# One level product and one score matrix for both directions of a gated scan, in a whole-network kernel on Trainium2

## The reference

```python
def step(S, xs):
    qc, kc, vc, gc = xs
    b = jnp.cumsum(gc, axis=2)
    decay = jnp.exp(jnp.where(lower, b[:, :, :, None, :] - b[:, :, None, :, :], -jnp.inf))
    a = jnp.einsum('bhtk,bhtsk,bhsk->bhts', qc, decay, kc)
    o = jnp.einsum('bhts,bhsv->bhtv', a, vc) + jnp.einsum('bhtk,bhkv->bhtv', qc * jnp.exp(b), S)
    ...
o_f, s_fwd = chunked_gated_scan(q, k_f, v, lf_f, s_fwd)
o_b, s_bwd = chunked_gated_scan(q[:, ::-1], k_b[:, ::-1], v[:, ::-1], lf_b[:, ::-1], s_bwd)
return o_f + o_b[:, ::-1], s_fwd, s_bwd
```

## Time and profile before

| | before |
|---|---|
| median of 3 runs | 3801.09 us (3799.83 to 3802.03) |
| the profiled execution | 3799.04 us, span 3797.2 us |
| TensorE (PE) busy | 3507.4 us, 92% of the span |
| VectorE (DVE) | 1810.3 us, 48% |
| ScalarE (ACT) | 1262.7 us, 33% |
| GpSimd (POOL) | 359.3 us, 9% |
| granted TensorE clock, mean | 0.958 |
| scan stage | about 1229 to 1855 us of the span |

### The profile page before, as it was taken

How to read it: one execution, slowest core, us unless ns; L and a number is a source line. 1 busy time by engine, 2 the same in 40 slices (tenths; PEclk the granted TensorE clock), 3 DMA queues, 4 the chain that set the end, 5 groups by cost and what they waited for, 6 DMA issues and landing times.

```text
span 3797.2 us, 44325 instructions
## 1 busy us (share of the span) xinstructions
PE 3507.4 (92%) x17640; PEld 2915.7 (77%) x17640; DVE 1810.3 (48%) x2841; ACT 1262.7 (33%) x1955; POOL 359.3 (9%) x386
## 2 busy tenths in 40 slices
PE   4999988999998887888799999999989999999898
PEld 3777777888887776777678887887768778877686
DVE  4665657755524456655543333334333333343333
ACT  2444443212123344434332223333332333333322
POOL 1010011000001222322200000001100000001000
PEclk7999989999998998898799999999999999999999
DMA  4222203655621210110123322222212232222122
GB/s 166 81 59 66 64 22 100 196 190 197 192 78 47 65 40 29 39 39 23 39 92 95 95 89 96 72 73 83 73 51 94 88 99 70 72 84 72 51 97 86
DMA packets 108269, 319.30 MB, mean 84 GB/s; under 512 B 28192, under 2 KB 29728, under 8 KB 107552
## 3 DMA queue, kind: packets, MB, share of 16 engines
q1 hardware_dynamic: 108064, 316.46, 26.1%
HBM read 314.32 MB, written 2.10 MB: 83 GB/s over the span
## 4 chain that ended last, share of the span: by engine, by line
PE 83%; DVE 8%; ACT 4%; issue 3%; DMA 1%; POOL 0%; SPq 0%; DVEq 0%; ACTq 0%
PE bank L913 20%; PE bank L915 19%; PE bank L914 19%; PE bank L918 3%; PE bank L919 3%; PE bank L920 3%; PE bank L1049 3%; PE bank L998 1%; PE bank L1102 1%; DVE tmp L1540 1%; PE bank L1121 1%; PE bank L1131 1%; ACT L1159 1%; PE bank L986 1%; PE bank L1084 1%
## 5 line engine op out<-in xcount | busy, mean ns | idle before, releaser
L913 PE MATMUL bank<-h_high_lat,w_high 128*128 128x512 f32 x2752 | 1148.2, 417 | 68.8 <-DVE h_low_ctx L1546 35.6
L915 PE MATMUL bank<-h_high_lat,w_low 128*128 128x512 f32 x2752 | 1088.5, 396 | 0.0
L914 PE MATMUL bank<-h_low_lat,w_high 128*128 128x512 f32 x2752 | 1088.0, 395 | 0.0
L1494 DVE TENSOR_TENSOR w_low<-w_raw,w_high 128x1024 fp32r<-128x1024 f32 (+2 forms) x440 | 527.7, 1201 | 1138.2 <-ACT w_high L1179 1137.1
L1179 ACT CAST w_high<-w_raw 128x1024 fp32r<-128x1024 f32 (+2 forms) x440 | 451.0, 1027 | 1384.4 <-PE bank L915 861.1
L913 PEld LDWEIGHTS bank<-h_high_lat,w_high 128*128 128x128 f32 x2752 | 526.5, 191 | 187.2 <-issue 73.0
L915 PEld LDWEIGHTS bank<-h_high_lat,w_low 128*128 128x128 f32 x2752 | 525.6, 191 | 114.8
L914 PEld LDWEIGHTS bank<-h_low_lat,w_high 128*128 128x128 f32 x2752 | 527.9, 192 | 80.7 <-issue 8.2
L1506 DVE SCALAR_TENSOR_TENSOR ada_product<-w_raw,c_rows 128x1024 f32<-128x1024 f32 x192 | 246.5, 1284 | 63.9 <-DMA w_raw<-in_ada_w_dram 51.8
L918 PE MATMUL bank<-h_high_ctx,w_high 128*128 128x256 f32 x800 | 225.7, 282 | 0.0
L919 PE MATMUL bank<-h_low_ctx,w_high 128*128 128x256 f32 x800 | 225.4, 282 | 0.0
(11 more groups left out here) (250 smaller groups left out, 4512.0 us busy)
## 6 DMA issues: line engine op xcount, KB each, us to landing
w_raw<-in_w_in_dram SPq DMA_DIRECT2D x176, 512.0 KB, 3.5
w_raw<-in_ada_w_dram SPq DMA_DIRECT2D x88, 512.0 KB, 3.6
w_raw<-in_ffn_in_dram SPq DMA_DIRECT2D x88, 512.0 KB, 3.6
w_raw<-in_w_ada_dram SPq DMA_DIRECT2D x48, 512.0 KB, 4.4
w_raw<-in_hg_in_dram SPq DMA_DIRECT2D x40, 512.0 KB, 3.5
w_raw<-in_ffn_out_dram SPq DMA_DIRECT2D x32, 512.0 KB, 3.6
w_raw<-in_qkv_dram SPq DMA_DIRECT2D x24, 512.0 KB, 3.5
w_raw<-in_proj_ret_dram SPq DMA_DIRECT2D x16, 512.0 KB, 3.5
```

Source lines behind the costliest of these rows:

```text
L913: e.matmul(lat_b, a, h[:, k, :], start=start, stop=False)
L914: e.matmul(lat_b, a, l[:, k, :], start=False, stop=False)
L915: done = e.matmul(lat_b, b, h[:, k, :], start=False, stop=stop)
L1494: e.tensor_tensor(w_lo[n % 2][:, 0:w], raw[slot][:, 0:w], w_hi[n % 2][:, 0:w].bitcast(F32), ALU.subtract).then_inc(s_lo, 1)
```

## The change

The forward direction needs scores from an earlier to a later half of each block, the backward one from a later to an earlier half. The new `hg_x` therefore holds two 512-column parts: keys (forward keys in first halves, backward keys in second halves) and queries, each with its decay. One product of the two gives both directions' scores of a level, in 128 columns a chunk, and one mask takes both from it into one matrix `hg_a`. So there are seven levels where there were fourteen, each with four GpSimd differences (the same 256 columns), one exponential of 1024 columns, three multiplications (256, 256, 512), four 128-column products and one masked copy of 512 columns. The diagonal is made once, from the sum of the two key tensors (`hg_ks`, a new VectorE addition in `square1`), and `hg_o` multiplies `v` once. GpSimd's first level waits for both running sums. The masks are half as many and are loaded in two parts. The generator's parts are now 26, spread as if 24, so its last two come when the next head's starts, and `LAG`, `KHAT` and `STATE` are set anew.

```diff
-LAG = 5
-KHAT, STATE = (3, 9), (6, 12)
+LAG = 3
+KHAT, STATE = (2, 5), (4, 7)
...
             yield
-        jobs = [(d, li) for d in range(2) for li in range(len(LEVELS))]
-        for s in range(len(jobs) + LAG):
+        for s in range(len(LEVELS) + LAG):
             if s >= LAG:
-                self.ev("hg_a", i, *jobs[s - LAG])
-            if s < len(jobs):
-                self.ev("hg_df", i, *jobs[s])
-            if 1 <= s <= len(jobs):
-                self.ev("hg_fa", i, *jobs[s - 1])
+                self.ev("hg_a", i, s - LAG)
+            if s < len(LEVELS):
+                self.ev("hg_df", i, s)
+            if 1 <= s <= len(LEVELS):
+                self.ev("hg_fa", i, s - 1)
             if s == 1:
-                self.ev("hg_a", i, 0, -1)
-            if s == 8:
-                self.ev("hg_a", i, 1, -1)
...
-        self.interleave([self.hg_pieces(i) for i in range(HG_HEADS)], [(self.hg_mixer(i), 36) for i in range(HG_HEADS)], 5 * (KC - 1))
+        self.interleave([self.hg_pieces(i) for i in range(HG_HEADS)], [(self.hg_mixer(i), 24) for i in range(HG_HEADS)], 5 * (KC - 1))
...
-            hg_d = ring("hg_d", 2, [P, LAT], st)
-            hg_x = ring("hg_x", 4, [P, LAT], st)
+            hg_d = ring("hg_d", 2, [P, 2, LAT], st)
+            hg_x = ring("hg_x", 3, [P, 2, LAT], st)
+            hg_ks = sqr[1][:, 0:LAT]
...
-            hg_a = ring("hg_a", 2, [P, NCH, P], st)
+            hg_a = sb("hg_a", [P, NCH, P], F32, st)
...
                     e.dma_start(hg_reset[:, :], io["hg_reset"]).then_inc(s_reset, 16)
                     e.wait_ge(s_nl, low_before[2] + KC)
-                    for u in range(4):
-                        d, lo, n = u // 2, (0, 4)[u % 2], (4, 3)[u % 2]
-                        if u >= 2:
-                            e.wait_ge(s_hm, u - 1)
-                        words = tmp[u % 2][:, 0:n * P].bitcast(U32).rearrange("p (l t) -> p l t", t=P)
-                        e.dma_start(words, io["hg_masks"][:, d, lo:lo + n, :]).then_inc(s_hml[u % 2], 16)
+                    for u, (lo, n) in enumerate(((0, 4), (4, 3))):
+                        words = tmp[u][:, 0:n * P].bitcast(U32).rearrange("p (l t) -> p l t", t=P)
+                        e.dma_start(words, io["hg_masks"][:, lo:lo + n, :]).then_inc(s_hml[u], 16)
...
-                            done = e.matmul(b[:, cols], hg_k[(2 * i + d) % 3][:, cols], hg_q[i % 2][:, cols], start=True, stop=True)
+                            done = e.matmul(b[:, cols], hg_ks[:, cols], hg_q[i % 2][:, cols], start=True, stop=True)
                     else:
-                        job = NL * (2 * i + d) + li
-                        half = 1 - d
+                        job = NL * i + li
                         e.wait_ge(s_hx, job + 1)
                         for n in range(NCH):
-                            xs = hg_x[job % 4][:, n * P:(n + 1) * P]
-                            xt = xs.rearrange("p (b a s) -> p b a s", a=2, s=LEVELS[li])[:, :, half, :]
-                            done = e.matmul(b[:, n * P // 2:(n + 1) * P // 2], xs, xt, start=True, stop=True)
+                            cols = slice(n * P, (n + 1) * P)
+                            done = e.matmul(b[:, cols], hg_x[job % 3][:, 0, cols], hg_x[job % 3][:, 1, cols], start=True, stop=True)
                     done.then_inc(s_hpa, 1)
...
                         cols = slice(n * P, (n + 1) * P)
                         for d in range(2):
                             e.matmul(b[:, cols], hg_st[d][:, n, :], hg_qb[d][:, cols], start=d == 0, stop=False)
-                            done = e.matmul(b[:, cols], hg_vt[:, n, :], hg_a[d][:, n, :], start=False, stop=d == 1)
+                        done = e.matmul(b[:, cols], hg_vt[:, n, :], hg_a[:, n, :], start=False, stop=True)
                     done.then_inc(s_hgo, 1)
...
                         e.tensor_scalar(t[:, :], t[:, :], TINY, None, ALU.max).then_inc(s_hft, 1)
+                    if i > 0:
+                        e.wait_ge(s_ha, ha_last[i - 1])
+                    e.wait_ge(s_hkk, 2 * i + 2)
+                    e.tensor_tensor(hg_ks[:, :], hg_k[2 * i % 3][:, 0:LAT], hg_k[(2 * i + 1) % 3][:, 0:LAT], ALU.add).then_inc(s_hks, 1)
...
-                    if job >= 4:
-                        was, li4 = divmod(job - 4, NL)
-                        e.wait_ge(s_hpa, nth[("hg_a", was // 2, was % 2, li4)])
+                    _, i, li = ev
+                    job = NL * i + li
+                    x, dl = hg_x[job % 3], hg_d[job % 2]
+                    if job >= 3:
+                        e.wait_ge(s_hpa, nth[("hg_a", *divmod(job - 3, NL))])
                     e.wait_ge(s_hde, job + 1)
-                    e.tensor_tensor(xv[:, :, 0, :], dv[:, :, 0, :], s1[:, :, 0, :], ALU.mult)
-                    e.tensor_tensor(xv[:, :, 1, :], dv[:, :, 1, :], s2[:, :, 1, :], ALU.mult).then_inc(s_hx, 1)
+                    e.wait_ge(s_hkk, 2 * i + 2)
+                    for a in range(2):
+                        e.tensor_tensor(hg_half(x[:, 0, :], li, a), hg_half(dl[:, 0, :], li, a), hg_half(hg_k[(2 * i + a) % 3], li, a), ALU.mult)
+                    e.tensor_tensor(x[:, 1, :], dl[:, 1, :], hg_q[i % 2][:, :], ALU.mult).then_inc(s_hx, 1)
                 elif kind == "hg_a":
-                    _, i, d, li = ev
-                    b, at = mix_bank[(ev, 0)], hg_a[d]
+                    _, i, li = ev
+                    b = mix_bank[(ev, 0)][:, :].rearrange("p (n t) -> p n t", t=P)
...
-                            e.wait_ge(s_hm, 4)
-                        e.wait_ge(s_ha, hg_before[ev])
+                            e.wait_ge(s_hm, 2)
+                        e.wait_ge(s_ha, nth[ev] - 1)
                         e.wait_ge(s_hpa, nth[ev])
-                        e.copy_predicated(to, mk.unsqueeze(1).broadcast_to([P, NCH, P // 2 // m, m]),
-                                          b[:, 0:LAT // 2].rearrange("p (n b s) -> p n b s", n=NCH, s=m)).then_inc(s_ha, 1)
+                        e.copy_predicated(hg_a[:, :, :], hg_mask[:, li:li + 1, :].broadcast_to([P, NCH, P]), b).then_inc(s_ha, 1)
                 elif kind == "hg_rd":
...
+                    _, i, li = ev
+                    job, m = NL * i + li, LEVELS[li]
+                    dk, dq = hg_d[job % 2][:, 0, :], hg_d[job % 2][:, 1, :]
+                    blocks = [P, LAT // (2 * m), m]
+                    bf, bb = ([hg_half(hg_b[d], li, a) for a in range(2)] for d in range(2))
+                    ref_f = bf[0][:, :, m - 1:m].broadcast_to(blocks)
+                    ref_b = bb[1][:, :, 0:1].broadcast_to(blocks)
                     if li == 0:
-                        e.wait_ge(s_hb, 2 * i + d + 1)
+                        e.wait_ge(s_hb, 2 * i + 2)
                     if job >= 2:
                         e.wait_ge(s_hx, job - 1)
-                    e.tensor_tensor(dv[:, :, 0, :], *p1, ALU.subtract)
-                    e.tensor_tensor(dv[:, :, 1, :], *p2, ALU.subtract).then_inc(s_hd, 1)
+                    e.tensor_tensor(hg_half(dk, li, 0), ref_f, bf[0], ALU.subtract)
+                    e.tensor_tensor(hg_half(dq, li, 1), bf[1], ref_f, ALU.subtract)
+                    e.tensor_tensor(hg_half(dk, li, 1), ref_b, bb[1], ALU.subtract)
+                    e.tensor_tensor(hg_half(dq, li, 0), bb[0], ref_b, ALU.subtract).then_inc(s_hd, 1)
```

70 lines of the change are left out of this document (22 added, 48 removed).

## The result

| | before | after |
|---|---|---|
| median | 3801.56 us (4 runs, 3799.83 to 3806.07) | 3712.38 us (4 runs, 3711.68 to 3712.99) |
| profiled execution | 3799.0 us | 3712.8 us |
| one head, seven of them, sum | 525.3 us | 443.8 us |
| last value piece to the next stage's first weight subtraction | 62.3 us | 58.7 us |
| granted clock, mean | 0.958 | 0.966 |

The ratio is 0.9764, 95% interval 0.9747 to 0.978: 89 us saved, where I had forecast 99, a time of 3702 and a range of 3683 to 3730. The forecast holds, 10 us off its middle.

A forecast was written before the change was run, and what follows sets the result against it. TensorE, busy for 92% of the span, and its waits were taken to bound the kernel. Savings of 90 us in seven heads, 6 in the last scan and 3 at the stage's start sum to 99: 3702 us, range 3683 to 3730.

The forecast's parts named there:

- first part: Head up to its first level's product, set by the ScalarE, VectorE and GpSimd chain: from 25.6 to 28.0 us.
- second part: Head from its first level's product on, set by TensorE's own work: from 49.5 to 33.5 us at full clock.
- clock loss: Time lost in a head to the clock falling in TensorE's waits: 0.8 us, a value near the low end.
- seven heads: Scans beside the next head's weights: 62.3 us each, 12.8 less, 90 us saved for seven.
- last scan: The eighth scan, running alone: 6 us saved, with ends of 3 and 9.
- start of the stage: Two mask loads and no wait let the next weights issue earlier: 3 us saved, bounds 1 and 3.2.
- (5) of the first part: GpSimd starts after both scans and has two levels ready before ScalarE is free for them: costs nothing.
- the readout: Its product now comes two steps into the next head, so the sigmoids and the chain start 1.7 us later.
- the three multiplications: First level's operands on VectorE: two operations of 0.41 and one of 0.68 replace two of 0.41, 0.7 us more.
- The rival (low as long as now): Clock stays low after the first level: 2.3 us a head more, 16 in all, 3718 us; chance 20%.
- GpSimd's pace: GpSimd's 5.8 us a level sets the second part: 3770 us, chance 4%; or slower, about 3840, chance 3%.
- the price of columns: A 128-column level costs twice a 64-column one: 5.7 us more a head, 40 in all, 3742 us; chance 3%.

The follow-up runs named there:

- run 1: Changed kernel with the output product and readout's product two slots earlier, before the next head starts, as in the kernel before; 3705.69 us.
- run 8: Kernel before the change with the first direction's key transposes one slot later; 3805.63 us, a single run.
- run 3: Changed kernel with each level's four products made twice over, same results; 3754.54 us.
- run 5: Changed kernel with products nobody reads added ahead of TensorE's four waits in seven heads, to hold the clock up; 3703.39 us.
- run 4: Changed kernel with GpSimd's second level held back until VectorE has made the last decayed queries; 3722.34 us.
- run 6: Changed kernel with both the output and readout products two slots earlier and unread products added ahead of TensorE's waits; 3700.1 us.
- run 2: Changed kernel with 64 of the 128 columns in every level's product, so the scan's output is wrong; 3717.28 us.
- run 11: Kernel before the change with unread products, 56 ahead of the first key transposes and 12 ahead of the first level, in seven heads; 3795.59 us.
- run 7: Changed kernel with the SP queue waiting for GpSimd's cast of both mask loads before issuing the next weights; 3714.51 us.
- run 10: Changed kernel with two further 128 KB mask loads ahead of the next weights and no wait; 3712.82 us.
- run 12: Changed kernel with the SP queue waiting between its two mask loads until GpSimd has cast the first; 3713.8 us.

## Why the prediction was right, and where it was off

The split held: a first part set by the chain (run 1 moved it by exactly the readout's 1.86 us, run 8 could not move it by TensorE's order), a second part set by TensorE (run 3), a clock loss (run 5). That the total is only 10 us off is helped by errors of both signs in the table. The saving of the profiled execution is 86.2 us for 99 forecast; the 12.8 between them:

| term | forecast | measured | how |
|---|---|---|---|
| first part of a head | 28.0 | 28.7 | mean of 26.85 and six of 29.06 |
| second part at full clock | 33.5 | 33.7 | 33.64 in the first head, 33.75 in run 5 |
| clock, a head | 0.8 | 1.0 | 34.67 on average, less 33.7 |
| seven heads | -90 | -81.5 | 525.3 to 443.8 |
| last scan | -6 | -3.6 | 62.3 to 58.7 |
| start of the stage | -3 | -4.7 | 41.1 to 36.4 |
| ahead of the stage | 0 | +3.5 | the mark at 1229.8, was 1226.3 |

- **The step that failed** is (5) of the first part, GpSimd has two levels ready early, "so nothing". Its eight operations stretch VectorE's chain by 1.36 us, which sets the first level: run 4 takes 1.28 of it away. The other steps of a steady head fit: 1.85 for the readout (1.7 forecast), 0.65 for the three multiplications (0.7), 0 for the key sum and the moved subtraction, and -0.37 that I hadn't seen, since GpSimd no longer runs beside the scans (3.50 us for 3.88). 25.57 + 1.85 + 1.36 + 0.65 - 0.37 = 29.06.
- **The second part** was right by luck: errors that cancel. The readout's product is worth 1.0 us, not 0.5 (runs 1, 5 and 6), and a level 0.81, not 0.86 (run 2), 0.4 over seven; the clock cost the head before 2.6 us, not the 3.1 that I took out (run 11). That makes 33.1, and a wait of 0.66 us for the second level, which I hadn't, 33.8.
- **The clock**: "a value near the low end" was right, 1.0 for 0.8. My reason, a gap ahead of the level that is nearly filled, was not: the clock is back at 1.00 between the waits (1537 to 1546), so the work there doesn't stretch into the last one; TensorE stands for 3.8 us ahead of the level, the clock falls, and two levels run at half clock. What keeps the loss small is that the wait for the second level would take the first of it anyway, and that the clock is back 2.9 to 6.2 us behind the level's start. The rival (low as long as now) was true in two of seven heads. The size is partly chance: runs 7, 10 and 12 leave the heads alone, and their seven sum to 447.0, 445.1 and 444.1 us for 443.8.
- **The last scan**: the output product starts 48.85 us after the value piece, not 45.8. The first level is at 26.8 for my 26, the same contention; the five levels of GpSimd that follow take 3.4 us each (1736.74 to 1750.27 for four) and not 3.1, which is 1.5; the masked copies wait behind. Behind it 1.7 us were saved for my 0.9.
- **The start**: the weights are cast 3.3 us earlier, as forecast, and TensorE's wait of 3.2 us is 0.46. With it the third piece's start at half clock went (0.80 us for a product, now 0.50), worth some 1.4 more. My reason, the wait, was half of it: put back alone it costs 0.7 to 0.8 (runs 7 and 12), since the loads ahead have then landed; the kernel before had a second pair of mask loads behind its wait and right ahead of the weights, and only the two together cost 3.3.
- **Ahead of the stage** nothing was changed. The mark lies at 1226.3, 1228.9 and 1229.6 in three profiles of the kernel before and its variants, and at 1227.2 to 1231.1 in eleven of the changed one and its variants, so such a difference comes between executions.

The other rivals are out: GpSimd's pace (run 3) and the price of columns (run 2).

## What to carry to other kernels

When two-input work moves to another engine or to another time, look at which chain it will then lie beside: an operation that is early and awaited by nobody can still lengthen the chain that sets the end, and that belongs in the sum and not only among the rivals. Price a low clock by heads of one trace that have it and heads that don't, not by half of the low time: at full clock part of it becomes a wait. And where products have their own weight loads, merging them pays by their number and hardly by their columns.
